# The state-space scan beside the weight stream: three products at a time, and one direction at a time

## The reference, cut to what matters

```
p = xn @ w_in[l]
z, xbc, dt_raw, p_rwkv, p_hgrn, p_gate = split(p)
y_ssm = ssd_branch(z, xbc, dt_raw, ...) @ w_branch_ssm[l]
...
# ssd_branch: the same scan forward, and backward on flipped inputs
y = y_f + y_b + xs * d_skip
# ssd_chunked, in 4 chunks of 128 positions, 16 heads of 64, state 128:
a_cum = cumsum(dt * a)                       # within the chunk
y_diag = (cm bm^T * exp(seg)) (x * dt)       # inside the chunk
state  = exp(a_cum[-1]) * state + bm^T (x * dt * decay_to_end)
y_off  = (cm state_before) * exp(a_cum)
```

## Time and profile before

| | |
|---|---|
| median of three runs | 3626.97 us (3622.23 to 3629.33) |
| profiled execution, span | 3630.0 us |
| TensorE busy | 3419.6 us, 94% |
| VectorE busy | 2100.3 us, 58% |
| ScalarE busy | 1326.7 us, 37% |
| mean granted TensorE clock | 0.974 of full |

### The profile page before, as it was taken

How to read it: one execution, slowest core, us unless ns; L and a number is a source line. 1 busy time by engine, 2 the same in 40 slices (tenths; PEclk the granted TensorE clock), 3 DMA queues, 4 the chain that set the end, 5 groups by cost and what they waited for, 6 DMA issues and landing times.

```text
span 3630.0 us, 56071 instructions
## 1 busy us (share of the span) xinstructions
PE 3419.6 (94%) x23384; PEld 2802.8 (77%) x23384; DVE 2100.3 (58%) x3889; ACT 1326.7 (37%) x2454; POOL 65.0 (2%) x32
## 2 busy tenths in 40 slices
PE   7999999999999999999999998998888989989999
PEld 6777688788888677788788886766677778778887
DVE  6776644544457677634544357663666688564434
ACT  4456443342234565443322223222332234232222
POOL 0000000000000000000000000000000033000000
PEclk9999999999999999999999989999999999899999
DMA  4221123233333221223233332324110324233332
GB/s 134 82 63 50 53 76 110 87 94 98 99 120 100 77 57 53 65 74 124 82 94 98 99 95 73 87 87 144 46 30 21 125 67 139 76 116 99 94 98 87
DMA packets 353827, 315.37 MB, mean 87 GB/s; under 512 B 11348, under 2 KB 281812, under 8 KB 353576
## 3 DMA queue, kind: packets, MB, share of 16 engines
q1 hardware_dynamic: 352712, 309.56, 28.5%
q10 hardware_dynamic: 864, 2.23, 0.2%
HBM read 288.15 MB, written 23.59 MB: 86 GB/s over the span
## 4 chain that ended last, share of the span: by engine, by line
PE 74%; DVE 16%; ACT 5%; issue 3%; DMA 2%; POOL 0%; SPq 0%; DVEq 0%; ACTq 0%; POOLq 0%
PE banks L524 12%; PE banks L526 12%; PE banks L525 12%; PE banks L427 8%; PE banks L429 8%; PE banks L428 8%; DVE weights_r L368 2%; PE banks L3092 2%; PE banks L624 1%; PE banks L2616 1%; ACT weights_high_r L361 1%; PE banks L2635 1%; PE banks L1107 1%; PE banks L1094 1%; ACT probabilities L1243 1%
## 5 line engine op out<-in xcount | busy, mean ns | idle before, releaser
L368 DVE TENSOR_TENSOR weights_r<-weights,weights_high_r 128x1024 fp32r<-128x1024 f32 (+3 forms) x520 | 606.8, 1175 | 468.8 <-ACT weights_high_r L361 467.9
L524 PE MATMUL banks<-h_T_hi,weights_high_r 128*128 128x512 f32 (+2 forms) x1904 | 760.0, 399 | 29.8 <-DVE h_T_lo L871 15.2
L526 PE MATMUL banks<-h_T_hi,weights_r 128*128 128x512 f32 (+2 forms) x1904 | 737.8, 387 | 0.0
L525 PE MATMUL banks<-h_T_lo,weights_high_r 128*128 128x512 f32 (+2 forms) x1904 | 737.5, 387 | 0.0
L361 ACT ACTIVATE weights_high_r<-weights 128x1024 fp32r<-128x1024 f32 (+3 forms) x520 | 510.4, 992 | 391.7 <-DMA weights<-in_w_mlp 219.1
L524 PEld LDWEIGHTS banks<-h_T_hi,weights_high_r 128*128 128x128 f32 x1904 | 362.7, 190 | 116.5 <-issue 38.5
L526 PEld LDWEIGHTS banks<-h_T_hi,weights_r 128*128 128x128 f32 x1904 | 362.1, 190 | 72.0
L525 PEld LDWEIGHTS banks<-h_T_lo,weights_high_r 128*128 128x128 f32 x1904 | 362.9, 191 | 69.3 <-issue 3.6
L427 PE MATMUL banks<-weights_high_r,h_T_hi 128*128 128x512 f32 (+3 forms) x704 | 290.3, 412 | 12.9 <-DVE h_T_lo L871 8.8
L429 PE MATMUL banks<-weights_high_r,h_T_lo 128*128 128x512 f32 (+3 forms) x704 | 266.2, 378 | 0.0
L428 PE MATMUL banks<-weights_r,h_T_hi 128*128 128x512 f32 (+3 forms) x704 | 265.8, 378 | 0.0
(11 more groups left out here) (571 smaller groups left out, 5478.9 us busy)
## 6 DMA issues: line engine op xcount, KB each, us to landing
weights<-in_w_in SPq DMA_DIRECT2D x182, 512.0 KB, 3.8
weights<-in_w_mlp SPq DMA_DIRECT2D x128, 512.0 KB, 3.8
weights<-in_ffn_w_in SPq DMA_DIRECT2D x44, 512.0 KB, 3.8
weights<-in_w_out SPq DMA_DIRECT2D x24, 512.0 KB, 3.6
weights<-in_ffn_w_down SPq DMA_DIRECT2D x22, 512.0 KB, 3.4
weights<-in_w_mem_kv SPq DMA_DIRECT2D x16, 512.0 KB, 3.6
weights<-in_w_diff_o SPq DMA_DIRECT2D x16, 512.0 KB, 3.7
weights<-in_w_mla_o SPq DMA_DIRECT2D x8, 512.0 KB, 3.4
```

Of the source, the lines that this page charges most:

```text
L368: ve.e.tensor_tensor(self.part(c.w_raw_r, u), self.part(c.w_raw, u), self.part(c.w_high_r, u).bitcast(F32), ALU.subtract).then_inc(*ve.tel ...
L524: pe.e.matmul(out, lhsT=wh[:, k, :], rhs=hi[k][:, cols], start=(k == 0), stop=False)
L525: pe.e.matmul(out, lhsT=wh[:, k, :], rhs=lo[k][:, cols], start=False, stop=False)
L526: mm = pe.e.matmul(out, lhsT=wl[:, k, :], rhs=hi[k][:, cols], start=False, stop=(k == self.chunks - 1))
```

## The change

Stream steps of "shift", "z" and "gates 0" are now one chunk (three matmuls) and half a unit long, so the last step of a tile stands at 3.5 of its four units and not at 3. The scan's step is split by direction: `by_direction` gives d = 0 and d = 1 steps of their own, so there are 57 steps, at 1 + 2.07 i, d = 0 at odd i and d = 1 at even i. TensorE's copy of a scan step still stands one unit behind. The instructions and their waits are the same; only their order within each engine's list differs.

```
--- before.py
+++ after.py
@@ -224,6 +224,7 @@
 
 
     n = 0
+    pace = 1
 
     def idle(self):
         for _ in range(self.n):
@@ -245,8 +246,8 @@
 
     def products(self, *jobs):
         for job in jobs:
-            self.at(job, range(self.now, self.now + job.n))
-            self.now += job.n
+            self.at(job, [self.now + n * job.pace for n in range(job.n)])
+            self.now += round(job.n * job.pace)
 
     def at(self, stage, times, later=0):
 
@@ -387,19 +388,22 @@
 
 
 
-    def __init__(self, c, tag, xT, chunks, src, sink, ready=(), tiles=NT, ring="gemm", together=NT, tile_ready=lambda t: ()):
+    def __init__(self, c, tag, xT, chunks, src, sink, ready=(), tiles=NT, ring="gemm", together=NT, tile_ready=lambda t: (), each=2):
         self.c, self.tag, self.xT, self.chunks, self.sink, self.ready, self.tiles = c, tag, xT, chunks, sink, ready, tiles
         self.ring, self.cols, self.tile_ready = ring, src.shape[1], tile_ready
         self.units = c.stream.tokens(src)
         self.passes = [range(t, min(t + together, tiles)) for t in range(0, tiles, together)]
-        self.n = len(self.units) * tiles
+        self.cuts = {u: [range(j, min(j + each, part)) for j in range(0, part, each)]
+                     for u in self.units for part in (c.stream.high(u).shape[1],)}
+        self.n, self.pace = tiles * sum(len(cuts) for cuts in self.cuts.values()), each / 2
 
     def steps(self):
 
         for n, some in enumerate(self.passes):
             for u in self.units:
                 for t in some:
-                    yield n, u, t, t == some[0], u == self.units[-1]
+                    for js in self.cuts[u]:
+                        yield n, u, t, js, t == some[0] and js is self.cuts[u][0], u == self.units[-1] and js is self.cuts[u][-1]
 
     def pe(self):
         c, pe = self.c, self.c.pe
@@ -407,7 +411,7 @@
         k0 = {}
         for u in self.units:
             k0[u] = sum(c.stream.high(v).shape[1] for v in self.units if v < u)
-        for n, u, t, first, final in self.steps():
+        for n, u, t, js, first, final in self.steps():
             wh, wl = c.stream.high(u), c.stream.low(u)
             part = wh.shape[1]
             if first:
@@ -419,9 +423,9 @@
                     pe.wait_all(self.ready)
             tok = slice(t * P, (t + 1) * P)
             pe.wait_all(self.tile_ready(t))
-            bank = c.fill(self.tag, t, ring=self.ring) if u == self.units[0] else c.slots[(self.tag, t)]
+            bank = c.fill(self.tag, t, ring=self.ring) if u == self.units[0] and js[0] == 0 else c.slots[(self.tag, t)]
             out = bank[:, 0:self.cols]
-            for j in range(part):
+            for j in js:
                 k = k0[u] + j
                 last = k == self.chunks - 1
                 pe.e.matmul(out, lhsT=hi[k][:, tok], rhs=wh[:, j, :], start=(k == 0), stop=False)
@@ -429,7 +433,7 @@
                 mm = pe.e.matmul(out, lhsT=lo[k][:, tok], rhs=wh[:, j, :], start=False, stop=last)
             if final:
                 mm.then_inc(*pe.tell("filled", self.tag, t))
-            if t == self.tiles - 1:
+            if t == self.tiles - 1 and js[-1] == part - 1:
                 if final:
                     c.values[("used", u)] = c.values[("filled", self.tag, t)]
                 else:
@@ -448,7 +452,7 @@
         return min(far, self.c.stream.reach(u if n == len(self.passes) - 1 else self.units[0]))
 
     def sp(self):
-        for n, u, t, first, final in self.steps():
+        for n, u, t, _, first, final in self.steps():
             if first and (n == len(self.passes) - 1 or u == self.units[0]):
                 self.c.stream.sp(u)
             if final:
@@ -492,15 +496,15 @@
 
 
 
-    def __init__(self, c, tag, xT, chunks, src, sink, ready=(), first=0, ring="gemm", late=None):
-        self.ring = ring
+    def __init__(self, c, tag, xT, chunks, src, sink, ready=(), first=0, ring="gemm", late=None, each=2):
+        self.ring, self.pace = ring, each / 2
         self.c, self.tag, self.xT, self.chunks, self.sink = c, tag, xT, chunks, sink
         self.units = list(enumerate(c.stream.features(src), first))
         if late:
             most = (NT - 1) * P
             self.parts = [(slice(0, most), 2, [mark for t in range(NT - 1) for mark in late.done(t)]), (slice(most, S), 4, late.done(NT - 1))]
         else:
-            self.parts = [(slice(0, S), 2, ready)]
+            self.parts = [(slice(0, S), each, ready)]
         self.n = len(self.units) * sum(chunks // each for _, each, _ in self.parts)
 
     def steps(self):
@@ -2113,6 +2117,19 @@
         yield
 
 
+def by_direction(*parts):
+
+    parts = [list(parts[d::2]) for d in range(2)]
+    while any(parts):
+        for own in parts:
+            for part in list(own):
+                try:
+                    next(part)
+                except StopIteration:
+                    own.remove(part)
+            yield
+
+
...
@@ -2266,7 +2283,7 @@
         halves = lambda x: [x[:, j * 512:(j + 1) * 512] for j in range(2)]
         self.own = [{"xdt": c.wide_cells(at, 2), "xend": c.wide_cells(at + 2, 2), "terms": halves(c.wide_cells(at + 4, 2)),
                      "dec": halves(c.wide_cells(at + 6, 2)), "add": c.cell(M + 5 + d)} for d, at in enumerate((E, Z))]
-        self.n = 1 + 7 * NT
+        self.n = 1 + 14 * NT
 
     def steps_pe(self):
         c, pe, k = self.c, self.c.pe, self.k
@@ -2486,20 +2503,20 @@
     def pe(self):
         yield
         for n in range(NT):
-            yield from rounds(self.chunk_pe(0, n), self.chunk_pe(1, n))
+            yield from by_direction(self.chunk_pe(0, n), self.chunk_pe(1, n))
         self.c.pe.stamp("ssm scan")
 
     def act(self):
         yield
         for n in range(NT):
-            yield from rounds(self.chunk_act(0, n), self.chunk_act(1, n))
+            yield from by_direction(self.chunk_act(0, n), self.chunk_act(1, n))
         self.c.ac.stamp("ssm scan")
 
     def dve(self):
         self.start_dve()
         yield
         for n in range(NT):
-            yield from rounds(self.chunk_dve(0, n), self.chunk_dve(1, n))
+            yield from by_direction(self.chunk_dve(0, n), self.chunk_dve(1, n))
         self.c.ve.settle()
         self.c.ve.stamp("ssm scan")
 
@@ -3571,18 +3588,19 @@
         scan_at = plan.now + 0.5
         staging = Staging(c, [*c.p, *c.gate], [*ssm.conv.done(), ("conv_tanh", 11)])
         shift = ShiftOut(c, k, staging, lambda f: c.kept["shift"][f * P:(f + 1) * P, :], ssm.conv.done())
-        plan.products(*(Features(c, "shift", c.hT, KD, w[:, C_RW + f * P:C_RW + (f + 2) * P], shift, ready=normed, first=f, ring=ring)
+        plan.products(*(Features(c, "shift", c.hT, KD, w[:, C_RW + f * P:C_RW + (f + 2) * P], shift, ready=normed, first=f, ring=ring, each=1)
                         for f in range(0, 14, 2)))
 
-        def kept_features(tag, col, n, how):
+        def kept_features(tag, col, n, how, each=2):
             sink = KeptOut(c, tag, range(n), staging, lambda f: c.kept[tag][f * P:(f + 1) * P, :], how)
-            return [Features(c, tag, c.hT, KD, w[:, col + f * P:col + (f + 2) * P], sink, ready=normed, first=f, ring=ring) for f in range(0, n, 2)]
-
-        def kept_tokens(tag, name, col, at, how):
+            return [Features(c, tag, c.hT, KD, w[:, col + f * P:col + (f + 2) * P], sink, ready=normed, first=f, ring=ring, each=each)
+                    for f in range(0, n, 2)]
+
+        def kept_tokens(tag, name, col, at, how, each=2):
             sink = KeptOut(c, name, range(NT), staging, lambda t: c.kept[tag][t * P:(t + 1) * P, at:at + 512], how)
-            return Tokens(c, name, c.hT, KD, w[:, col:col + 512], sink, ready=normed, ring=ring, together=2)
-        plan.products(*(kept_tokens("z", f"z {h}", C_Z + h * 512, h * 512, "silu") for h in range(2)))
-        gates = lambda first, n: kept_features(f"gates {first}", C_G2 + first * P, n, "tanh")
+            return Tokens(c, name, c.hT, KD, w[:, col:col + 512], sink, ready=normed, ring=ring, together=2, each=each)
+        plan.products(*(kept_tokens("z", f"z {h}", C_Z + h * 512, h * 512, "silu", 1) for h in range(2)))
+        gates = lambda first, n: kept_features(f"gates {first}", C_G2 + first * P, n, "tanh", 2 if first else 1)
         plan.products(*gates(0, 8))
         plan.beside(ssm, scan_at, plan.now - 1.5, 1)
         y_kept = Fetch(c, "y out", [(c.kept["y"].rearrange("(t p) d -> p t d", p=P), ssm.y)], all_at("ssm scan"))
```

44 lines of the change are left out of this document (23 added, 21 removed).

## The result

The kernel after the change takes 3643.17 us (median of five runs, 3639.53 to 3648.34). Five runs of the kernel before give 3629.33 us. The ratio is 1.0043 with a 95% interval of 1.0032 to 1.0054 (the two medians alone give 1.0038): slower by 0.43%, where the forecast was 3631 and "no difference that can be measured".

The account below looks back on a forecast made before the run. VectorE's end of the scan was taken to decide the time. Losses of 30.7 us after against 28.5 before gave +2.2, with the end's 1.7 +3.9: span 3633.9, median 3631 us, range 3611 to 3643.

Parts of the forecast that it names:

- What bounds the scan, and what follows it: VectorE's end of the scan decides the time; store 7.95 us and read 11.02 us follow, TensorE waits 7.4 us.
- The rival in which the end swallows the difference: Behind the scan: the chain begins with something other than VectorE's end, hiding gain or loss; 3627 us, chance 0.12.
- The pattern and the six waits: Beside shift, chunks 0 and 1: TensorE reaches direction 0's steps before VectorE's L2424; six waits, 12.9 us together.
- The start: Scan's start: direction 0's s0 work stands ahead of the first tile's pads on VectorE; bank wait grows from 1.5 to 3.3 us.
- The first wait: q0 of direction 0, scan's start: TensorE waits 4.5 us for VectorE's L2424, against 5.2 before.
- The end: Scan's end: x1 of direction 1 stands two units later, with a shorter VectorE tail; +1.7 us, nothing changes behind it.
- Direction 1: q3 of chunks 1 to 3: three waits, 7.3 us, go; one of 0.75 comes at i = 8; total under 2 us.
- "z" and "gates": In z the bank wait shrinks from 1.9 to 0.95 us, three new ones come: 3.65 in all, against 8.6 before.
- Clock and switches: Over the scan: slow clock after waits costs 4.8 us (2.5 plus 2.3), extra stream-to-scan switches 0.8 us.
- a remainder before: Scan stretch before: 256.0 less 148.9 stream and 78.6 scan steps leaves 28.5 us waiting and slow clock; waits name 18.6.
- the finer steps win: Rival: the six direction 0 waits don't come, as VectorE is further ahead; 3615.7 us, or 3608.7; chance 0.25.
- A clock held at half for half of 80 us: Rival: two-microsecond waits between 2275 and 2355 keep the clock low, 20 us instead of 2.3; 3648.6 us, chance 0.13.

Follow-up runs that it names:

- after_light: The changed kernel without the token shift's two VectorE additions per tile, keeping only the scaled copy: 3629.85 us, ratio 0.9998 to the kernel before.

## Why the prediction was wrong

*What bounds the scan, and what follows it: right.* In every kernel the span behind the scan's last addition is 1130.5 to 1138.9 us, while the scans differ by 27 us; so the scan's end decides the time, but for these 8 us, which I can't assign. The chain of store and read is there each time. The rival in which the end swallows the difference is refuted.

*The pattern and the six waits: right.* Priced at 12.9 us in all (1.9, 2.2, 2.7, 2.4, 1.7, 2.0), measured 10.9 idle (1.75, 2.02, 2.48, 2.21, 1.09, 1.35), at the steps named; with the 0.26 us that each costs on top it is 12.5. after_light shows the cause. *The start: right in its sum.* The bank wait was priced at 3.3 and is 1.4; the other 1.5 is the wait of L2372 for VectorE's L662, which I hadn't seen and which TensorE would otherwise probably have spent at the bank. The first wait is 4.34 (4.5). *The end: right.* x1 of direction 1 comes 3.63 us behind that of direction 0 (2504.11 to 2507.74), and priced was 2.73 + 0.86 = 3.59. *Direction 1:* the three waits of 2.1 to 2.6 are gone as said, for two short ones beside shift (0.41 and about 0.7, priced 0.75 in one), but 3.6 us are left and not under 2.

*"z" and "gates", 3.65 us: too small.* The bank waits of z came to 4.84 us instead of 3.65. Beside the gates I had nothing, and four waits of direction 1 (0.36 still in z, 1.16, 0.48, 0.48) make 2.5. I had checked the distance from tile to scan step for the pattern with VectorE's three shift instructions, and took the gates, whose tile ScalarE alone takes out, for free; that ScalarE's copy holds the high half, and with it VectorE's list, I didn't walk. Together 7.3 instead of 3.65.

*Clock and switches, 5.6 us against what before had: the step that failed.* All idle time of TensorE after was forecast as 25.1 us and is 26.5. Against the 18.6 of the table before that alone is +7.9 us. The forecast made +2.2 of the losses because it set the items after (25.1 + 4.8 clock + 0.8 switches = 30.7) against a remainder before (28.5, found by subtraction). In that remainder were 9.9 us without a name, slow clock and hand-overs at each step, and I let them shrink to 5.6. They did not: with 13.4 us for the scan, of which the end is 1.7, the losses rose by 11.7, to 40.2 by the same account. Of these 26.5 are idle, and 13.7 stand where I had 5.6. A loss of +7.9 in waits, +1.7 at the end and nothing won in the remainder would have given 3636.6 from the median of 3627, and with the measured +3.8 in the remainder 3640.4. That the switches are free is right (0.8 priced, 0 found).

Most of the two remainders can be named. Every wait costs 0.26 us beyond its idle time (shown above). With 16 waits before that is 4.2 us, with 20 waits after 5.2; the forecast had no term for it. The clock stood at half for two stretches before, 13.65 us, of which TensorE worked 10.57 (7.16 and 3.41), and for four of 3.4 us after, in all of which it worked:

```profile
2256.41:2266.65 10.24, 7.16 (x23) 5.74 (x24) 4.22 (x6) 0.60 (x1) 0.00 (x0) 0.50 0.27 77
2355.40:2358.81 3.41, 3.41 (x10) 2.12 (x9) 0.35 (x1) 0.00 (x0) 0.00 (x0) 0.50 0.00 0
```
```profile
2253.95:2257.37 3.42, 3.42 (x13) 2.94 (x13) 3.38 (x5) 0.00 (x0) 0.00 (x0) 0.50 0.30 82
```

The first two rows are the two of the kernel before, the third is the first of the four after. At half speed half of the worked time is lost: an estimate of 5.3 us before and 6.8 after, where 4.8 was priced. Before, the clock had fallen while TensorE still waited (at 2256.41, in the wait from 2254.25 to 2259.49) and not after the wait, as the prediction says, so 3.1 us of the low stretch cost nothing. Together these two make 9.5 of the 9.9 us before and 12.0 of the 13.7 after, so of the 3.8 they give 2.5; the other 1.3 stay open.

```profile
2232.90:2506.41 273.51, 248.34 (x1081) 183.71 (x1082) 165.24 (x229) 65.66 (x94) 0.00 (x0) 0.98 0.29 84
2276.60:2283.00 6.40, 6.39 (x25) 4.99 (x25) 2.30 (x3) 0.00 (x0) 0.00 (x0) 0.73 0.40 106
2323.80:2330.00 6.20, 6.20 (x23) 4.81 (x24) 1.12 (x2) 0.00 (x0) 0.00 (x0) 0.72 0.16 60
2336.80:2343.00 6.20, 6.15 (x34) 5.03 (x34) 1.20 (x2) 0.63 (x2) 0.00 (x0) 1.00 0.19 71
2440.00:2446.00 6.00, 5.63 (x14) 3.28 (x15) 3.45 (x7) 0.00 (x0) 0.00 (x0) 0.72 0.59 175
```

These are further stretches of the kernel after, with the columns of the earlier trace rows; the granted clock is the third value from the end. Behind the wait that ended at 2336.85 it stays at full, behind those that ended at 2276.61 and 2323.77 it does not.

*The rivals.* That the finer steps win is refuted by the six waits. A clock held at half for half of 80 us is refuted as well: over 2274 to 2362 the mean granted clock is 0.96, against 0.98 over the matching stretch before, which is some 2 us. That rival named the right side for another reason. The rule that I weighed, frequent micro-idles that drive the clock back and forth (the Trainium skill, "TensorE: Matmul & The Clock Gate", section "A second HAM failure mode: psum-queue depth-cycling"), is seen here only as single low stretches behind some waits: with nearly twice as many alternations the mean clock of the scan is 0.98, as before (0.97).

*The band.* A chance of 0.54 for "same" was high for a forecast whose own sum had 9.9 us without a name in it: that remainder is larger than the 7.3 us that tell slower from same.

## What to carry to other kernels

Where two jobs share in-order engines, what a new order costs isn't the number of steps but which instruction stands directly ahead of the one that the bound engine waits for; walk every kind of tile on every engine, also the one whose output seems to touch only another engine. When a difference is forecast, hold the same items against each other before and after, and keep an unnamed remainder as it is, or find out what it is made of. And when a wait comes from one misplaced instruction, move that one: swapping it with its neighbour won 8 us where splitting the whole schedule lost 13.

## What the runs showed of the hardware that was not expected

- A run of eight small matmuls and a 512-column product between stream matmuls costs the same alone or in pairs (1.76 against 3.52 us for two), so a switch costs 0.02 us or less.
- A wait of TensorE costs 0.26 us more than the idle time that the profile shows for it, whether this is 0.15 or 2.5 us.
- The granted clock doesn't follow a wait by its length alone. After idle times of 1.75 and 2.48 us it fell (0.73 and 0.72 over the next six microseconds), after 2.02 and 2.21 it was 1.00 throughout; in the kernel before, a wait of 2.58 us at 2354.99 had 0.83 behind it and one of 2.58 at 2424.53 had 1.00 over ten microseconds.
- Two halves of one change cost 6.4 and 13.0 us alone and 13.4 together: effects of place don't add.
